# A block of the in-projection stored once, as 128x1024, instead of twice, as 128x512

## The reference

```python
ada = c @ w_ada + b_ada
shift, scale, gate = jnp.split(ada, 3, axis=-1)
h = _layer_norm(x) * (1.0 + scale) + shift          # 1024 x 2048
proj = h @ w_in                                      # 2048 x 10760
(fq, fk, fv, flog, sq, sk, sv, g_fox, g_swa, m_fox, m_swa) = jnp.split(proj, SPLIT_IDX, axis=-1)
o_fox = _forgetting_attention(fq, fk, fv, flog, b_f)       # 8 heads of 128
o_swa = _sliding_window_attention(sq, sk, sv, sinks)       # 16 query heads of 64, window 128
y_fox = (o_fox * silu(g_fox)) @ w_br_fox
y_swa = (o_swa * silu(g_swa)) @ w_br_swa
merged = sigmoid(m_fox) * y_fox + sigmoid(m_swa) * y_swa
x = _layer_norm(ALPHA * x + gate * (merged @ w_out)) * ln_g + ln_b
```

## Time and profile before

| | us |
|---|---|
| median of three executions | 2814.3 |
| the profiled execution | 2818.61 |
| its span, first to last instruction | 2816.9 |
| PE busy in it | 2663.5 |
| DVE busy | 1822.4 |
| ACT busy | 1141.0 |
| POOL busy | 252.5 |

### The profile page before, as it was taken

One profiled execution on the slowest core, in us unless ns is written; L12 is line 12 of the kernel. 1 busy time (PEld: TensorE's weight loads), 2 busy tenths in 40 slices (PEclk: granted clock), 3 DMA queues, 4 the chain that ended last, 5 costly groups with the idle time before them and its releaser, 6 DMA issues.

```text
span 2816.9 us, 39170 instructions
## 1 busy us (share of the span) xinstructions
PE 2663.5 (95%) x12161; PEld 2171.4 (77%) x12161; DVE 1822.4 (65%) x2965; ACT 1141.0 (41%) x2088; POOL 252.5 (9%) x281
## 2 busy tenths in 40 slices
PE   5799999999999999999989999999978999999995
PEld 2478887787877888888868888888857888888884
DVE  6856667786657777787776666666664455644345
ACT  5433335333325555454554444444443332334211
POOL 0000000112120000000001111111100010024003
PEclk9899999999999999999999999999999999999997
DMA  7556773576663334433455545544564455556442
GB/s 274 187 187 217 207 218 105 136 178 153 165 137 93 114 117 117 118 117 117 153 156 126 116 111 119 126 107 111 112 192 142 141 183 179 160 164 193 158 135 103
DMA packets 328893, 418.49 MB, mean 149 GB/s; under 512 B 20392, under 2 KB 231400, under 8 KB 325104
## 3 DMA queue, kind: packets, MB, share of 16 engines
q1 hardware_dynamic: 286144, 343.04, 38.6%
q0 software_dynamic: 29616, 66.12, 12.6%
q10 hardware_dynamic: 13056, 8.39, 1.1%
HBM read 297.90 MB, written 119.59 MB: 148 GB/s over the span
## 4 chain that ended last, share of the span: by engine, by line
PE 83%; DVE 6%; ACT 4%; issue 3%; DMA 3%; POOL 1%; SPq 0%; ACTq 0%; DVEq 0%; POOLq 0%
PE pA L1769 18%; PE pD L1769 16%; PE pC L1769 16%; PE zP L2429 12%; PE yP L2375 11%; PE tP L1675 2%; PE sP L1907 1%; PE oP L1930 1%; DVE w_sum L1223 1%; PE sP L1737 1%; DMA b_lo<-b_scratch 1%; DMA w_raw<-in_w_br_fox_dram 1%; PE oP L1932 1%; ACT sp_w L992 1%; ACT w_hi L838 1%
## 5 line engine op out<-in xcount | busy, mean ns | idle before, releaser
L1228 DVE TENSOR_TENSOR w_lo<-w_sum,w_hi 128x512 fp32r<-128x512 f32 x336 | 230.3, 688 | 186.8 <-ACT w_hi L838 185.9
L1769 PE MATMUL pC<-b_hi,w_hi 128*128 128x512 f32 x784 | 312.2, 398 | 24.6 <-ACT ctile L852 20.6
L1769 PE MATMUL pA<-b_hi,w_hi 128*128 128x512 f32 x784 | 309.4, 395 | 5.8 <-DVE w_lo L1228 2.8
L1769 PE MATMUL pD<-b_hi,w_hi 128*128 128x512 f32 x784 | 306.7, 391 | 3.7 <-ACT ctile L852 3.7
L1769 PE MATMUL pC<-b_hi,w_lo 128*128 128x512 f32 x784 | 310.0, 395 | 0.0
L1769 PE MATMUL pC<-b_lo,w_hi 128*128 128x512 f32 x784 | 308.6, 394 | 0.0
L1769 PE MATMUL pA<-b_lo,w_hi 128*128 128x512 f32 x784 | 308.4, 393 | 0.0
L1769 PE MATMUL pA<-b_hi,w_lo 128*128 128x512 f32 x784 | 307.7, 392 | 0.0
L1769 PE MATMUL pD<-b_lo,w_hi 128*128 128x512 f32 x784 | 305.3, 389 | 0.0
L1769 PE MATMUL pD<-b_hi,w_lo 128*128 128x512 f32 x784 | 305.3, 389 | 0.0
L171 ACT CAST w_hi<-w_raw 128x1024 fp32r<-128x1024 f32 x128 | 134.9, 1054 | 413.5 <-PE zP L2429 211.1
(11 more groups left out here) (268 smaller groups left out, 5048.5 us busy)
## 6 DMA issues: line engine op xcount, KB each, us to landing
w_raw<-in_w_in_dram SPq DMA_DIRECT2D x168, 512.0 KB, 5.7
proj_scratch<-ctile SPq DMA_DIRECT2D x168, 256.0 KB, 2.2
proj_scratch<-ctile POOLq DMA_DIRECT2D x168, 256.0 KB, 6.0
bg_raw<-in_w_ada_dram SPq DMA_DIRECT2D x64, 512.0 KB, 4.0
w_raw<-in_w_out_dram SPq DMA_DIRECT2D x64, 512.0 KB, 3.7
w_raw<-in_w_br_swa_dram SPq DMA_DIRECT2D x32, 512.0 KB, 4.2
aux<-proj_scratch SPq DMA_DIRECT2D x64, 256.0 KB, 3.9
w_raw<-in_w_br_fox_dram SPq DMA_DIRECT2D x32, 512.0 KB, 3.9
```

The lines of the kernel that those rows point to most:

```text
L1228: nc.vector.tensor_tensor(ring(k, True), factor(k), ring(k, False).bitcast(F32), ALU.subtract).then_inc(in_lo, 1)
L1769: last = nc.tensor.matmul(bank(r, k)[:], w[:, j, :], b[:, j, :], start=(k < 4 and n == 0), stop=(n == 11), skip_group_check=True)
```

## The change

Each block is stored or added by one transfer of 128x1024, 512 KB. The transfer of row 0 is issued where tile 3's was, after product 5, and reads tile 1 too. The transfer of row 1 is issued where tile 4's was, after product 6, and reads tile 2 too. Tile 1's own transfer after product 1 is gone, and so is tile 2's. Tiles 1 and 3 share one semaphore, and so do tiles 4 and 2.

```diff
-            stored = {n: sem(f"stored_tile_{n}") for n in TILES}
-            added = {n: sem(f"added_tile_{n}") for n in TILES}
+            stored = {n: sem(f"stored_tile_{n}") for n in (3, 4)}
+            added = {n: sem(f"added_tile_{n}") for n in (3, 4)}
+            for group_of in (stored, added):
+                group_of[1], group_of[2] = group_of[3], group_of[4]
...
-            def tile_of(dst, n):
-
-                row, half = TILE_AT[n]
-                return proj_d[ds(dst + row, 1), :, half * HALF:(half + 1) * HALF].rearrange("a p t -> p (a t)")
+            def block_of(dst, n):
+
+                return proj_d[ds(dst + TILE_AT[n][0], 1), :, :].rearrange("a p t -> p (a t)")
...
                 def store(q, n, g):
 
-                    if n != 2:
+                    if n in (3, 4):
                         tile_done(sp, q, n)
-                    sp.dma_start(tile_of(2 * g, n), tiles[n]).then_inc(stored[n], 16)
+                        sp.dma_start(block_of(2 * g, n), ctile[:, TILE_AT[n][0], :]).then_inc(stored[n], 16)
...
                 def add_tile(q, n, dst):
 
-                    tile_done(pool, q, n)
-                    pool.dma_start(tile_of(dst, n), tiles[n], accum_op=ALU.add).then_inc(added[n], 16)
+                    if n in (3, 4):
+                        tile_done(pool, q, n)
+                        pool.dma_start(block_of(dst, n), ctile[:, TILE_AT[n][0], :], accum_op=ALU.add
+                                       ).then_inc(added[n], 16)
```

## The result

| | us |
|---|---|
| changed kernel, median of 18 executions | 2823.4 (2819.9 to 2828.2) |
| kernel before, beside it, median of 18 | 2816.45 (2813.2 to 2820.5) |
| ratio | 1.0025, 95% interval [1.0018, 1.0032] |

The change costs 7 us, between 5.1 and 9.0. The prediction of 2814.0, in a range of 2809 to 2822, was wrong: the time moved up, and past the end of the range. The profiled execution took 2824.98 us, its span is 2823.2.

The account below looks back on a forecast made before the run. PE was taken as the bound, busy 2663.5 of 2816.9 us, so transfers count only where PE waits. The terms 0 + 0 - 1.0 + 0 - 0.3 + 0 + 1.0 = -0.3 us gave a median of 2814.0, range 2809 to 2822.

Parts of the forecast that it names:

- The transfers: Landing times of 512 KB from `ctile`: store 3.1 us, lone add 5.3, row-1 add 7.4 from the first issue.
- Stage A, 0: 18 groups: 36 issues on SP removed, takes of tiles 1 and 4 come after the stores land; cost 0.
- Stage B, 0: 18 groups: ACT waits 1.9 us at tile 1 and 1.2 at tile 4, hidden by its idle time; cost 0.
- From B to C, -1.0: Transition to stage C: one issue for both tiles lands 1.0 us sooner and shortens PE's 2.88 us wait.
- Stage C, 0: 24 groups: tile 1's take waits 1.9 us for its store in one group in three at most; cost 0.
- its rival: Stage C loses at tile 1's take, 8 groups times some 0.6 us, 5 us: 2819; chance 0.10.
- third rival: Stage C's repeating 2.0 us wait per pair of token blocks goes, up to 16 us faster: 2798; chance 0.06.
- From C to D, -0.3: Transition to stage D: tile 1's store leaves the queue ahead of a 1 MB load; 0.3 us gained.
- Stage D, 0: 24 groups: tile 4's take comes 7.3 us after issue against 7.4, delay absorbed up to 8.0; cost 0.
- The first rival: Row add lands late, PE waits at tile 4's take in stage D's eight heads, 11 us: 2826; chance 0.10.
- After D, +1.0: After stage D: tile 1's last 256 KB moves into full DMA engines, 1.6 us, less 0.6 for a saved issue.
- The rule of the Trainium skill: Queues alternate by whole packets, so weight loads beside a 512 KB add would land up to 1.6 us later.

Follow-up runs that it names:

- e1: Kernel before with only the stores of stages A and C merged to 512 KB, adds left tile by tile; between -2.5 and +2.5 us against before.
- e7: Changed kernel with most of DVE's forget-gate operations in groups 20 to 24 cut to 8x8 elements; 3.1 us slower than before.
- e11: Changed kernel with the gate row's small transfer issued between the row-0 and row-1 adds of group 26; +2.3 us against before (-0.3 to +4.5).
- e2: Kernel before with only the adds of stage B merged, both rows; 4.8 us slower than before (2.3 to 7.3).
- e4: Kernel before with only row 1 (tiles 4 and 2) merged, in all four stages, first series; 2.3 us faster than before.
- e4b: Kernel before with only row 1 merged in all four stages, timed again in a second series; 2813.79 us, 3.4 us faster than before.
- e10: Changed kernel with the last group's four tiles added by four 256 KB transfers; median 0.5 us below the changed kernel's, interval 4.2 to 10.1 us against before.
- e12: Kernel before with row 1 alone merged and the gate row's transfer issued before the row-1 add of group 26; 2813.82 us.
- e3: Kernel before with only the adds of stage D merged, both rows; 3.7 us slower than before (1.1 to 6.2).
- e5: Kernel before, all transfers 256 KB, but in stage B tile 1's add issued with tile 3's after product 5; 4.8 us slower than before.
- e6: Kernel before with most of DVE's forget-gate operations in groups 20 to 24 cut to 8x8 elements; +1.4 us against before (-1.4 to +3.9).
- e8: Kernel before with only row 0 (tiles 1 and 3) merged, in all four stages; 1.7 us slower than before (-0.8 to +4.2).

## Why the prediction was wrong, step by step

- **The transfers.** Right. The row-0 adds issued at 580.41 and 658.18 land after 5.4 us (forecast 5.3); the row-1 add issued at 583.45 after 7.6 (forecast 7.4). The forecast 7.4 holds with 3 us between the two issues. With 1.8 between them, at 640.64 and 659.96, the second takes 8.8.
- **Stage A, 0.** Right, 0.3 in the profile and e1's ratio of 1.0000.
- **Stage B, 0, "PE sees nothing; ACT's idle time is what hides it", bounds -1 and +2.** This is the step that failed. The 30 waits for the adds came as forecast, but in groups 23 to 26 they are longer, 3.2 to 3.5 us and 2.7 to 3.2 instead of 1.9 and 1.2: I had taken the row-0 add to be issued when tile 3's was before, and it is up to 2.0 us later. And PE lost time before the delay of tile 4's take had reached the 3.5 us of room that I had worked out. I followed the take to the product that needs the copy and no further. Behind tile 4's take stands a weight copy, and behind this DVE, whose queue is in order and 75% full in groups 23 to 26 (58.24 us of 78 in the changed kernel); that DVE is late in some groups I had put into the bounds without working out what it costs. The loss is 1.5 us in those groups (e7 shows that it hangs on DVE's load, and groups 28 to 34, with DVE 62% full, lose nothing). It also had to be asked what else stands in the queue behind the moved bytes: the gate row, which I had not named. It costs 2.15 us and then 1.6 of clock (e11, which moves only this row, loses neither). Together 5.3 us, against a bound of +2.
- **From B to C, -1.0, bounds -2.9 and 0.** The direction is right and the size too low. The kernels whose row-1 add of stage B is merged gain 3.1 us on average between groups 35 and 37 (change, e2, e4, e4b, e7, e10, e11, e12), those where it isn't 0.9 (before, with 0, and e1, e3, e5, e6, e8): 2.2. Each of these figures is of one execution and holds its clock.
- **Stage C, 0, and its rival.** Right: tile 1's take waits 1.4 to 1.5 us more in four of the 24 groups and 1.0 in one, and e1 is not slower. The wait of 2.0 per pair that a third rival spoke of is still there, 19.0 us in 16 waits against 20.6 in 15.
- **From C to D, -0.3.** -0.7 in the profile, but e1 with the same stores shows +0.3; not to be told.
- **Stage D, 0, bounds 0 and +5.6.** The row-1 add issued at 1538.60 lands after 7.8 us, just under the 8.0 at which I said the chain of the head begins to lose, and the profile shows 0.5 us for the stage, no more than kernels with the old adds there show. The first rival (11 us) falls. e3 is 3.7 us slower all the same, and 1.9 of this come at the end of the program.
- **After D, +1.0.** Right for the chain's start: the store takes 0.9 longer, and the loads start 0.8 later relative to PE's last group. PE's last matmul is 0.7 later than at the end of stage D.
- **The end of the program, for which the sum has no term.** This is the second step that failed. The prediction ends with the loads of the closing stage and puts nothing behind them, without a reason. POOL's `DRAIN` takes 2.04 us longer, and the program ends after it. In the five kernels with both rows of stage D merged it is 1.9 to 2.3 us longer, in the four with one row 0.5, in the others not at all; why is open.
- **The rule of the Trainium skill** ("DMA: Bandwidth & Descriptors", "Queues, rings and completion order"), by which the weight load beside a 512 KB add is delayed. The load's median went from 5.7 to 6.2 us to landing. That is the direction of the delay, and a third of the 1.6 allowed. But in e5, all of whose adds are of 256 KB, it is 6.3, so no run here ties it to the size, and no wait of DVE for `w_raw` came of it from 540 to 660 us. The Trainium skill, on this page, counts a packet in descriptors; that twice the bytes of a transfer make a load stand behind twice the bytes was my step, and nothing here shows it.

The forecast's sum with the measured terms is 5.3 (B) - 2.2 + 0.8 + 2.0 (the end of the program) = +5.9, inside the interval of 5.1 to 9.0. The 0.3 of stage A and the 0.5 of stage D, which can't be told from nothing, would make it 6.7.

The kernels with row 1 alone (e4, e4b, e12) are the fastest here, 2813.8 us each. e4b and e12 are 3.4 us under the kernel before by the ratio (0.8 to 5.9), and 9.6 under the changed one, which was timed in another series.

## What to carry to other kernels

When a transfer is made later or longer and an engine's idle time seems to cover the wait, follow the work behind that wait through every engine, to the last thing queued in order behind it: here ACT's idle time covered the wait, but DVE stood behind ACT's next instruction, and DVE had no time to give. Ask also which small transfers sit in the same queue behind the larger one, and who waits for them. And merge the pieces that become ready together (row 1, after product 6); one that is ready four products sooner than its neighbour is better sent at once. When the places where PE falls behind don't add up to the time, look behind the last matmul: here 2 of 7 us lay there, in an instruction that no engine's busy time shows.

## What the runs showed of the hardware

- A 4 KB transfer lands with what is ahead of it in its queue: the gate row of group 26 lands 0.2 to 1.2 us behind the last add, in all 12 profiles in which it is issued behind it. That is 8.2 us after its own issue in the changed kernel, 8.5 in e7 and only 5.7 in e4. Issued before this add it takes 5.4 us (e11) and 4.0 (e12). The Trainium skill says on its page "DMA: Bandwidth & Descriptors", "Two DMAs through the same engine are not ordered", that descriptors within a queue of a DMA engine start in order; this agrees.
- The `DRAIN` at the end of POOL's program takes 6.60, 7.13 or 8.5 to 8.9 us, by how many rows of stage D's adds are merged (0, 1 or 2), in 14 profiles without an exception. The program ends 0.24 us after it.
- One wait of 2 to 3 us of PE can cost more than itself: in four of five kernels with such a wait at 673 us the granted clock was 0.50 for the 3.4 us behind it, another 1.6 us. In the kernels with a wait of 1.0 or less there, it wasn't. It is no rule: at group 36 PE waits 2.5 us in e1 and 3.0 in e8, and neither has a half-clock stretch there.
- The half-clock stretches differ between executions by several of 1.6 us, which is the size of what was looked for here; the lateness of single products places a loss to 0.1 us, while the span of one profile doesn't tell 3 us.
